# The dilated-group attention stage of a decoder step, unrolled and with plain fp32 matmuls for scores and values

## The chip, the cores and the metric

The kernel runs on one core of one Trainium2 chip. The metric is the device time of one execution in microseconds (us). Most executions of this kernel agree within 0.3%.

## The reference, cut to what matters

One step of a decoder trunk with two layers: a prompt of 2048 tokens of width 1024 and eight sample rows. Layer 0 is a gated short convolution beside attention to a memory; layer 1 is attention with three dilated windows beside attention to a memory. All is float32. The change touches the three dilated windows of the prompt. For each group (window 128 with stride 1, 512 with stride 4, 2048 with stride 16), four heads of 128 columns:

```
qb = to_res(q)                 # tokens regrouped by residue mod d, in blocks of 128
kk = with_prev(to_res(k))      # previous block and own block
vv = with_prev(to_res(v))
s = einsum('brnqhe,brnkhe->brnhqk', qb, kk)
s = where(valid, s, NEG)       # banded and causal inside the two blocks
m = max(s); p = exp(s - m); l = sum(p)
o = einsum('brnhqk,brnkhe->brnqhe', p / l, vv)
```

The kernel stores the unnormalised sums, the maxima and the denominators per group; the output stage combines the three groups with them.

## The kernel before, in words

The program is a chain of stages, each ended by a barrier: `mix_stage` and `out_stage` for layer 0, then `shared_stage` (the projections to shared keys and values, queries and gates), `dil_stage` (the three groups) and `out_stage` for layer 1. In most stages a product of two fp32 tensors is made by `split3` (L107): each operand is kept as a high part (rounded to fp32r) and a low part (the rest), and three fp32r matmuls high x high (L109), high x low (L110) and low x high (L111) accumulate in PSUM.

`dil_stage` (L3060) goes over 48 tiles: three groups of 16 blocks of 128 queries, first the group of stride 16, then 4, then 1. A tile handles the four heads. With stride 16 every residue has a single block of keys, so each of its 16 tiles has one key block. With stride 4 the first block of each of the four residues has one, the other 12 tiles have two (the previous and its own). With stride 1 tile 32 has one and the other 15 have two. In all 21 tiles have one key block and 27 have two.

The work of a tile s is spread over steps, and every engine has its own order inside a step (`body`), written by hand:

- SP (L3177): loads q and k of tile s (4 buffers each, a slot is free when the tile four back was turned), then v of tile s - 1 (`load_v`, L3171).
- TensorE (`body`, L3461): `score` of tile s - 1, `turn` of tile s (four transpositions of q into PSUM bank 0 at L3429, four of k into bank 5 at L3432), `sums` of tile s - 3 (probabilities times values), `turn_probs` of tile s - 2 (L3457).
- ScalarE (L3260): copies the high part of the turned probabilities of s - 3 (L3254, two halves), copies the sums of s - 4 (L3247), copies the high parts of the turned q and k of s (L3267, L3268), exponentials of s - 1 (L3239).
- VectorE (L3341): low parts of the probabilities of s - 3 (L3322), adds the low half of the sums of s - 4 into the output (L3330), minima of s - 1 (scaled, masked scores with a running minimum, L3312), low parts of q and k of s (L3344, L3346).
- GpSimd (L3214): splits v of s into high and low (L3220, L3222; the low part sits beside the high part, so that one 256-column matmul gives both products), then issues the stores of the denominators of s - 2 (L3167) and the output of s - 4 (L3163).

`score` waits for both low parts of the turned q and k of its tile, so the chain turn, high copy, low subtraction, score stands between one turn and the next. `turns` (L3089) emits four bodies for the first four tiles of a group and a hardware loop with four bodies for the remaining twelve; `cnt`, `half_cnt` and `use` turn a tile into semaphore values. After the last tile, the stage already begins the first tile of the output stage: SP loads its rows (L3194 to L3199), TensorE turns its query (L3477) and makes its scores by `split3`, VectorE combines the groups (`next_groups_max` to `next_combine`).

In the decode part of the output stage a plain fp32 matmul (no fp32r) stands at L2328: eight weight columns by 512 columns, 24 times in the program, and at L2326 four times by 128 columns.

Of the kernel before, what the change touches and what calls it, by code (L numbers as in the profile page):

```python
# [3059 lines left out]
def dil_stage(core, q_src, kv_src, dst, front, ahead, ops_out):  # L3060
# [11 lines left out]
    def has_prev(g, q, u):  # L3072
        d = STRIDES[g]
        if NT // d == 1:
            return False
        if d > 1:
            return u > 0
        return not (isinstance(q, int) and q == 0 and u == 0)

    def rows(ap, g, q, u):  # L3080
        d = STRIDES[g]
        view = ap.rearrange("(m d) c -> d m c", d=d)
        if NT // d == 1:
            return view[ds(q * U + u, 1), :, :].rearrange("o m c -> (o m) c")
        if d > 1:
            return view[ds(q, 1), u * P:(u + 1) * P, :].rearrange("o m c -> (o m) c")
        return view[:, ds(q * (U * P) + u * P, P), :].rearrange("o m c -> (o m) c")

    def turns(eng, body):  # L3089
        for g in range(GROUPS):  # L3090
            for u in range(U):
                body(g, 0, u)
            with eng.Fori(1, TURNS) as q:
                for u in range(U):
                    body(g, q, u)

    def back(s, k):
        g, q, u = s
        if u >= k:
            return g, q, u - k  # L3100
        if isinstance(q, int) and q == 0:
            return (g - 1, TURNS - 1, u - k + U) if g else None
        return g, q - 1, u - k + U

    END = (GROUPS - 1, TURNS, 0)

    def cnt(s, per=1, extra=1):
        g, q, u = s
        return q * (U * per) + ((g * NT + u) * per + extra)

    def half_cnt(s, half):
        return cnt(s, 2, half + 1)

    def use(s, per=16):
        return s[1] * per + (s[0] * TURNS + 1) * per

    with ExitStack() as st:
        q_b, k_b, v_b = front.dil
        o_b, lse = front.o, front.lse
        o_out, l_out = front.o_out, front.l_out  # L3120
        qt_hi = core.sb(st, "dil_qthi", [P, C], F32R)
        qt_lo = core.sb(st, "dil_qtlo", [P, C], F32R)
        kt_hi = core.sb(st, "dil_kthi", [P, H, 2, P], F32R)
        kt_lo = core.sb(st, "dil_ktlo", [P, H, 2, P], F32R)
        v_hl = core.sb(st, "dil_vhl", [P, U, H, 2, HD], F32R)
        prob = core.sb(st, "dil_prob", [P, 2, H, 2, P])
        pt_hi = core.sb(st, "dil_pthi", [P, H, 2, P], F32R)
        pt_lo = core.sb(st, "dil_ptlo", [P, H, 2, P], F32R)
        zeros = core.sb(st, "dil_zeros", [P, C])
        scratch = core.sb(st, "dil_scratch", [P, 2 * U])  # L3130
        masks = core.sb(st, "dil_masks", [P, 3 * P])
        names = ("qk_in0 qk_in1 qk_in2 qk_in3 v_in0 v_in1 v_in2 v_in3 "
                 "zeroed masked turned qhi_done khi_done qlo_done klo_done vhi_done "
                 "vlo_done scored biased exped pturned phi_done plo_done summed o_begun o_done")
        sems = core.sems(st, "dil", names)
        qk_in, v_in = (sems[n * U:(n + 1) * U] for n in range(2))
        (zeroed, masked, turned, qhi_done, khi_done, qlo_done, klo_done, vhi_done, vlo_done, scored, biased, exped, pturned,
         phi_done, plo_done, summed, o_begun, o_done) = sems[2 * U:]
        block = st.enter_context(nc.Block())

        def keys(s):

            return (1 - s[2] % 2, s[2] % 2) if has_prev(*s) else (s[2] % 2,)

        def span(s):
            ks = sorted(keys(s))
            return ks[0], ks[-1] + 1

        def mask(s):
            if has_prev(*s):  # L3150
                return masks[:, 0:2 * P] if s[2] % 2 else masks[:, P:3 * P]
            return masks[:, P:2 * P]

        scores = ps[:, 1:3, :].rearrange("p a (b s k) -> p (a b) s k", b=2, s=2)
        sums_hl = ps[:, 6:8, :].rearrange("p a (b x e) -> p (a b) x e", b=2, x=2)
        turned_p = ps[:, 3:5, :].rearrange("p a (b s k) -> p (a b) s k", b=2, s=2)
        next_q = ps[:, 0, :].rearrange("p (h t) -> p h t", h=H)
        cstat = front.cstat
        groups = lambda n: cstat[:, n, :].rearrange("p (g h) -> p g h", h=H)

        def store(eng, s, landed=None):
            eng.wait_ge(o_done, cnt(s))
            eng.dma_start(rows(dst[s[0]][:, 0:C], *s), o_b[:, s[2], :]).then_inc(landed or o_out[s[2]], 16)  # L3163

        def store_lse(eng, s, landed=None):
            eng.wait_ge(exped, half_cnt(s, 1))
            eng.dma_start(rows(dst[s[0]][:, C:OW], *s), lse[:, s[2], :]).then_inc(landed or l_out[s[2]], 16)  # L3167

        @block.sync
        def _(sp):  # L3170
            def load_v(s):  # L3171
                g, _, u = s
                if back(s, U):
                    sp.wait_ge(vlo_done, cnt(back(s, U)))
                sp.dma_start(v_b[:, u, :], rows(kv_src[g][:, C:2 * C], *s)).then_inc(v_in[u], 16)

            def body(*s):  # L3177
                g, _, u = s
                if back(s, U):
                    sp.wait_ge(turned, cnt(back(s, U)))  # L3180
                sp.dma_start(q_b[:, u, :], rows(q_src[g], *s)).then_inc(qk_in[u], 16)
                sp.dma_start(k_b[:, u, :], rows(kv_src[g][:, 0:C], *s)).then_inc(qk_in[u], 16)
                if back(s, 1):
                    load_v(back(s, 1))
            turns(sp, body)
            load_v(back(END, 1))
            sp.wait_ge(turned, NT * GROUPS)
            sp.wait_ge(vlo_done, NT * GROUPS)
            for slot in range(U):
                sp.wait_ge(o_out[slot], 16 * ((GROUPS - 1) * TURNS + 1))  # L3190
                sp.wait_ge(l_out[slot], 16 * ((GROUPS - 1) * TURNS + 1))
# [8 lines left out]
            store_lse(sp, back(END, 1), front.last_out)  # L3200
            for k in (2, 1):
                store(sp, back(END, k), front.last_out)

        @block.gpsimd
        def _(pool):
            pool.memset(zeros[:, :], 0.0).then_inc(zeroed, 1)
            pool.memset(masks[:, :], 0.0).then_inc(zeroed, 1)
            pool.wait_ge(zeroed, 2)
# [4 lines left out]

            def body(*s):  # L3214
                u = s[2]
                pool.wait_ge(v_in[u], use(s))
                if back(s, 3):
                    pool.wait_ge(summed, cnt(back(s, 3)))
                v, zero = (t.rearrange("p (h e) -> p h e", h=H) for t in (v_b[:, u, :], zeros[:, :]))
# [3 lines left out]
                if back(s, 2):  # L3223
                    store_lse(pool, back(s, 2))
                if back(s, 4):
                    store(pool, back(s, 4))
# [6 lines left out]
        def _(act):  # L3233
# [9 lines left out]
            def copy_sums(s):  # L3243
                act.wait_ge(summed, cnt(s))
                if back(s, U):
                    act.wait_ge(o_out[s[2]], use(back(s, U)))
# [376 lines left out]
```

## Time and profile before

| | us |
|---|---|
| median of 3 runs | 2947.7 |
| lowest, highest run | 2941.38, 2948.47 |
| span of the profiled execution, first to last instruction | 2951.0 |

The profiled execution's own time is given by its span alone, 3.3 us above the median of the runs. Busy shares over the span: TensorE matmuls 96%, weight loads 78%, VectorE 63%, ScalarE 40%, GpSimd 16%. Matmuls are pipelined: a record of a matmul lasts longer than the distance to the next start, so work on TensorE is costed by the distance between starts, and a merged row (x4, x8) covers from the first start to the last end. The mean granted clock of TensorE is 0.981 of 2.4 GHz; 0.50 in a row is the 1.2 GHz level. Times in the trace count from the first instruction of the span. Kernels of other stages use the same lines L109 to L111, so groups are told apart by the tiles they read and write.

### The profile page before, as it was taken

How to read it: one execution, taken by the hardware profiler on the slowest of the kernel's cores; microseconds unless marked ns; L12 is line 12 of the kernel's file. 1: busy time of each engine (PE TensorE's matmuls, PEld its weight loads, DVE VectorE, ACT ScalarE, POOL GpSimd, SP SyncE). 2: the span in 40 equal slices, each digit the busy share in tenths (PEclk: the TensorE clock that was granted, in tenths of full speed). 3: DMA queues.
4: the chain of work that ended last, by engine and by line, in shares of the span. 5: the costliest groups of instructions: out<-in, count | busy, mean ns of one | idle time of the engine just before them, and what ended most of it. 6: DMA issues, size and time to landing. Idle time of an engine off the chain costs nothing. (4 is left out here: it accounts for less than half of the span.)

```text
span 2951.0 us, 40709 instructions
## 1 busy us (share of the span) xinstructions
PE 2819.4 (96%) x13910; PEld 2315.7 (78%) x13910; DVE 1855.2 (63%) x3966; ACT 1187.9 (40%) x3494; POOL 461.8 (16%) x614
## 2 busy tenths in 40 slices
PE   7999999999998999979999999999999979989999
PEld 6787888888776888868778788777777768887787
DVE  4585766666785543334656667665746658877765
ACT  5432221312243242234343536323223458866642
POOL 0001010101000000000110202323331157640000
PEclk9999999999998999989999999999999989999999
DMA  4285645555675343232565667887776756646542
GB/s 170 84 251 192 191 154 185 183 171 178 219 243 169 108 150 107 72 133 101 192 241 194 238 203 249 258 276 223 262 250 222 266 194 210 199 145 226 198 145 98
DMA packets 281059, 556.96 MB, mean 189 GB/s; under 512 B 30385, under 2 KB 80113, under 8 KB 280873
## 3 DMA queue, kind: packets, MB, share of 16 engines
q1 hardware_dynamic: 248552, 455.99, 47.2%
q0 software_dynamic: 32320, 98.60, 9.7%
q8 instruction: 103, 1.69, 0.2%
q14 instruction: 84, 0.68, 0.1%
HBM read 421.76 MB, written 132.72 MB: 188 GB/s over the span
## 5 line engine op out<-in xcount | busy, mean ns | idle before, releaser
L109 PE MATMUL ps<-b_wp,b_sring 128*128 128x512 f32 x640 | 252.5, 395 | 17.8 <-DMA b_sring<-sums_dram 13.9
L110 PE MATMUL ps<-b_wp,b_sring 128*128 128x512 f32 x640 | 251.5, 393 | 0.0
L111 PE MATMUL ps<-b_wp,b_sring 128*128 128x512 f32 x640 | 251.5, 393 | 0.0
L109 PE MATMUL ps<-a_sring,a_wp 128*128 128x512 f32 x512 | 199.9, 390 | 2.2 <-DMA a_sring<-sums_a_dram 2.2
L111 PE MATMUL ps<-a_sring,a_wp 128*128 128x512 f32 x512 | 199.4, 389 | 0.0
L110 PE MATMUL ps<-a_sring,a_wp 128*128 128x512 f32 x512 | 199.4, 389 | 0.0
L908 DVE TENSOR_TENSOR shared_o<-ps,b_spare 128x512 f32<-128x512 f32 x160 | 109.8, 687 | 133.9 <-PE ps L111 114.9
L111 PE MATMUL ps<-b_wp,b_xtlo 128*128 128x512 f32 x496 | 193.2, 389 | 0.0
L109 PE MATMUL ps<-b_wp,b_xthi 128*128 128x512 f32 x480 | 186.9, 389 | 0.5 <-ACT b_spare L852 0.5
L110 PE MATMUL ps<-b_wp,b_xthi 128*128 128x512 f32 x480 | 186.8, 389 | 0.0
L669 POOL DMA_DIRECT2D kv_dram<-shared_o x102 | 56.3, 552 | 748.0 <-DVE shared_o L893 605.9
L713 ACT ACTIVATE ps<-shared_o 128x128 f32<-128x128 f32 (+1 forms) x408 | 108.0, 265 | 148.5 <-DVE shared_o L908 144.5
L109 PEld LDWEIGHTS ps<-b_wp,b_sring 128*128 128x128 f32 x640 | 121.6, 190 | 48.8 <-issue 15.8
L109 PE MATMUL ps<-a_xthi,out_cathi 128*128 128x512 f32 x384 | 154.5, 402 | 1.7 <-DVE out_catlo L2790 1.7
L111 PE MATMUL ps<-a_xthi,out_catlo 128*128 128x512 f32 x384 | 150.4, 392 | 0.0
L110 PE MATMUL ps<-a_xtlo,out_cathi 128*128 128x512 f32 x384 | 150.1, 391 | 0.0
L110 PE MATMUL ps<-a_xtlo,a_wp 128*128 128x512 f32 x384 | 149.5, 389 | 0.0
L111 PE MATMUL ps<-a_xthi,a_wp 128*128 128x512 f32 x384 | 149.5, 389 | 0.0
L109 PE MATMUL ps<-a_xthi,a_wp 128*128 128x512 f32 x384 | 149.5, 389 | 0.0
L111 PEld LDWEIGHTS ps<-b_wp,b_sring 128*128 128x128 f32 x640 | 121.4, 190 | 25.7
L110 PEld LDWEIGHTS ps<-b_wp,b_sring 128*128 128x128 f32 x640 | 121.4, 190 | 25.1
L893 DVE SCALAR_TENSOR_TENSOR shared_o<-shared_o,shared_stat,shared_grow 128x128 f32<-128x128 f32 (+1 forms) x408 | 122.7, 363 | 3.6
(492 smaller groups left out, 7528.9 us busy)
## 6 DMA issues: line engine op xcount, KB each, us to landing
b_sring<-sums_dram SPq DMA_DIRECT2D x160, 512.0 KB, 5.1
a_sring<-sums_a_dram SPq DMA_DIRECT2D x128, 512.0 KB, 5.0
b_raws<-w_b_dram SPq DMA_DIRECT2D x176, 256.0 KB, 4.0
a_raws<-w_a_dram SPq DMA_DIRECT2D x140, 256.0 KB, 4.3
kv_dram<-shared_o POOLq DMA_DIRECT2D x96, 256.0 KB, 4.0
tok_b_dram<-shared_o POOLq DMA_DIRECT2D x96, 256.0 KB, 4.7
front<-tok_b_dram SPq DMA_DIRECT2D x96, 256.0 KB, 3.2
front<-kv_dram SPq DMA_DIRECT2D x96, 256.0 KB, 4.1
```

The costliest lines, as they stand in the source:

```text
L109: pe.matmul(acc, a_hi, b_hi, start=first, stop=False)
L110: pe.matmul(acc, a_hi, b_lo, start=False, stop=False)
L111: return pe.matmul(acc, a_lo, b_hi, start=False, stop=last)
L669: pool.dma_start(dst, o[0:n, i % RING, :]).then_inc(o_out[i % RING], 16)
L713: sq = act.activation(to[:, cols], of[:, cols], ACT.Square, accum_out=stat[0:n, slot, 0, h:h + 1])
L893: m = dve.scalar_tensor_tensor(out=o[0:n, slot, cols], in0=of[:, cols], scalar=stat[0:n, slot, 2, h:h + 1], in1=grow[0:n, g, cols], op0=AL ...
L908: dve.tensor_tensor(o[:, i % RING, :], product, with_acc, ALU.add).then_inc(o_done if kinds[i] == "copy" else added, 1)
```

## The change

The stage is written out: 48 tiles in Python, numbered 0 to 47, with constants for all semaphore values, no hardware loop. In it:

- The turned q is copied to SBUF once, as plain fp32, by ScalarE (`copy_query`, 2 slots), the turned k once by VectorE (`copy_keys`, 3 slots), the turned probabilities of heads 0 and 1 by ScalarE (`probs_first`) and of heads 2 and 3 by VectorE (`probs_second`). Values are used as loaded, in 8 buffers of their own.
- `score` is one fp32 matmul per head, over 128 or 256 columns, in place of three fp32r; `sums` one fp32 matmul over 128 columns per head and key block, in place of two fp32r over 256 and 128.
- GpSimd computes nothing but the masks, and issues the stores. VectorE no longer adds sums: ScalarE's copy gives the output, from a PSUM bank that alternates by tile.
- The order: scores two steps behind the turn (one before), probabilities turned three behind (two before), sums four behind (three before). The scores also wait for the minima of the tile before, and turning for the copies of the tile before.

The diff, cut to its core, in this order: sizes, buffers, SP's loads, GpSimd's value operations, the orders of ScalarE and of VectorE, a score, a sum, the order of TensorE:

```diff
-    U = 4
-    TURNS = NT // U
+    U, V, R = 4, 8, 3
+    TILES = NT * GROUPS
...
+        v_b = core.sb(st, "dil_v", [P, V, C])
+        qt = core.sb(st, "dil_qt", [P, 2, C])
+        kt = core.sb(st, "dil_kt", [P, H, R, P])
+        pt = core.sb(st, "dil_pt", [P, H, 2, P])
...
+            for s in range(TILES):
+                if s >= U:
+                    sp.wait_ge(turned, s - U + 1)
+                sp.dma_start(q_b[:, s % U, :], rows(q_src, s)).then_inc(qk_in[s % U], 16)
+                sp.dma_start(k_b[:, s % U, :], rows([x[:, 0:C] for x in kv_src], s)).then_inc(qk_in[s % U], 16)
+                if s >= V:
+                    sp.wait_ge(summed, s - V + 2)
+                sp.dma_start(v_b[:, s % V, :], rows([x[:, C:2 * C] for x in kv_src], s)).then_inc(v_in[s % V], 16)
...
-                pool.tensor_tensor(v_hl[:, u, :, 0, :], v, zero, ALU.add).then_inc(vhi_done, 1)
-                pool.wait_ge(vhi_done, cnt(s))
-                pool.tensor_tensor(v_hl[:, u, :, 1, :], v, v_hl[:, u, :, 0, :], ALU.subtract).then_inc(vlo_done, 1)
...
+            for s in range(TILES + 2):
+                if real(s - 4):
+                    probs_first(s - 4)
+                if real(s - 5):
+                    copy_sums(s - 5)
+                if real(s - 2):
+                    exps(s - 2, 0)
+                    exps(s - 2, 1)
+                if real(s):
+                    copy_query(s)
...
+            for s in range(TILES + 2):
+                if real(s - 4):
+                    probs_second(s - 4)
+                if real(s - 2):
+                    minima(s - 2, 0)
+                    minima(s - 2, 1)
+                if real(s):
+                    copy_keys(s)
...
+                pe.wait_ge(q_copied, s + 1)
+                pe.wait_ge(k_copied, s + 1)
+                if s:
+                    pe.wait_ge(biased, 2 * s)
...
-                    m = split3(pe, scores[:, h, a:b, :].rearrange("p s k -> p (s k)"), qt_hi[:, cols], qt_lo[:, cols],
-                               kt_hi[:, h, a:b, :].rearrange("p s k -> p (s k)"),
-                               kt_lo[:, h, a:b, :].rearrange("p s k -> p (s k)"), True, True)
...
+                    m = pe.matmul(scores[:, h, 0:n, :], qt[:, s % 2, cols], kt[:, h, at, :], start=True, stop=True)
...
-                        pe.matmul(sums_hl[:, h, :, :].rearrange("p x e -> p (x e)"), pt_hi[:, h, key, :],
-                                  v_hl[:, slot, h, :, :].rearrange("p x e -> p (x e)"), start=(j == 0), stop=False)
-                        m = pe.matmul(sums_hl[:, h, 0, :], pt_lo[:, h, key, :], v_hl[:, slot, h, 0, :],
-                                      start=False, stop=last)
+                        m = pe.matmul(sums_at(s)[:, h, :], pt[:, h, i, :], v_b[:, key % V, cols], start=(i == 0),
+                                      stop=(i == len(order(s)) - 1))
...
+            for s in range(TILES + 2):
+                if real(s - 2):
+                    score(s - 2)
+                if real(s):
+                    turn(s)
...
+                if real(s - 4):
+                    sums(s - 4)
+                if real(s - 3):
+                    turn_probs(s - 3)
```

## Rows read from the trace of the kernel before

**Rows 1.** The head of the page.

```profile
span 2951.0 us, 40709 instructions
```

**Rows 2.** TensorE's timeline (start us, length us): turns of tiles 0, 5, 18, 47; output stage.

```profile
2373.69 0.69 PE L3429 MATMUL ps<-ident,front 128*128 128x128 f32 x2 [8.73 <-DMA front<-kv_dram]
...
2403.60 0.29 PE L3429 MATMUL ps<-ident,front 128*128 128x128 f32 x1
...
2462.60 0.60 PE L3429 MATMUL ps<-ident,front 128*128 128x128 f32 x4
...
2617.21 0.60 PE L3429 MATMUL ps<-ident,front 128*128 128x128 f32 x4
...
2641.94 1.09 PE L2915 MATMUL ps<-ident,front_od 128*128 128x128 f32 x4 [4.14 <-PEq L3117]
```

**Rows 3.** Windows: length, busy PE, PEld, DVE, ACT, POOL, clock, DMA share, GB/s.

```profile
2374.00:2386.00 12.00, 7.72 (x36) 6.97 (x34) 3.59 (x14) 4.66 (x12) 7.54 (x6) 0.50 0.84 290
2404.00:2460.00 56.00, 49.32 (x400) 44.30 (x398) 44.01 (x192) 44.69 (x159) 44.09 (x50) 1.00 0.71 227
2537.00:2617.00 80.00, 75.84 (x640) 72.91 (x640) 65.68 (x225) 66.91 (x195) 52.32 (x58) 1.00 0.53 172
```

**Rows 4.** TensorE's timeline over one period of a one-block tile.

```profile
2424.87 0.30 PE L109 MATMUL ps<-dil_kthi,dil_qthi 128*128 128x128 f32 x1 [0.57 <-DVE dil_ktlo L3346]
...
2426.24 0.62 PE L3429 MATMUL ps<-ident,front 128*128 128x128 f32 x4
...
2427.28 0.36 PE L3446 MATMUL ps<-dil_vhl,dil_pthi 128*128 128x256 f32 x1
...
2428.23 0.61 PE L3457 MATMUL ps<-ident,dil_prob 128*128 128x128 f32 x4
2429.40 0.30 PE L109 MATMUL ps<-dil_kthi,dil_qthi 128*128 128x128 f32 x1 [0.56 <-DVE dil_ktlo L3346]
```

**Rows 5.** Waits from 2404 to 2460: total us, times, longest.

```profile
PEld ps L109 <- DVE dil_qtlo L3344: 9.2, 12, 0.8
```

**Rows 6.** Groups of 2376 to 2640 by form: count | busy us, mean ns | idle before.

```profile
L3268 ACT ACTIVATE dil_kthi<-ps 128x512 fp32r<-128x512 f32 x48 | 28.4, 592 | 0.0
L3254 ACT ACTIVATE dil_pthi<-ps 128x256 fp32r<-128x256 f32 x42 | 13.5, 374 | 0.0
L3322 DVE TENSOR_TENSOR dil_ptlo<-ps,dil_pthi 128x256 fp32r<-128x256 f32 x42 | 15.9, 420 | 20.8 <-ACT dil_pthi L3254 20.8
L3330 DVE TENSOR_TENSOR dil_o<-ps,dil_o 128x512 f32<-128x512 f32 x48 | 32.9, 686 | 0.1
L3220 POOL TENSOR_TENSOR dil_vhl<-front,dil_zeros 128x512 fp32r<-128x512 f32 x48 | 61.1, 1274 | 76.5 <-PE ps L3448 71.4 <-DMA front<-kv_dram 5.1
```

**Rows 7.** Plain fp32 matmuls of the decode part (L2328, L2326) beside fp32r matmuls.

```profile
L2328 PE MATMUL ps<-b_spare,dec_sel x24: 592/592/596, 2715.7 to 2848.2; 128*8 128x512 f32 x24
...
2715.70 1.88 PE L2328 MATMUL ps<-b_spare,dec_sel 128*8 128x512 f32 x4
...
2770.65 0.39 PE L109 MATMUL ps<-b_xthi,out_cathi 128*128 128x512 f32 x1
2770.89 0.40 PE L110 MATMUL ps<-b_xtlo,out_cathi 128*128 128x512 f32 x1
...
2772.40 1.04 PE L2326 MATMUL ps<-dec_nv,ident 32*8 32x128 f32 x8
```

**Rows 8.** TensorE's timeline in a two-block step: first sums, probabilities, next scores.

```profile
2618.22 0.35 PE L3446 MATMUL ps<-dil_vhl,dil_pthi 128*128 128x256 f32 x1
...
2620.10 1.05 PE L3457 MATMUL ps<-ident,dil_prob 128*128 128x128 f32 x8
2620.90 0.37 PE L109 MATMUL ps<-dil_kthi,dil_qthi 128*128 128x256 f32 x1
```

**Rows 9.** DMA of 2400 to 2450: GB/s in 40 equal slices, and the mean.

```profile
GB/s 7 252 326 70 164 306 324 57 246 377 216 138 259 333 115 173 343 321 30 259 362 195 164 282 375 25 215 369 256 12 123 328 347 97 167 369 244 202 249 372
DMA packets 5889, 11.34 MB, mean 227 GB/s; under 512 B 1031, under 2 KB 1031, under 8 KB 5886
```

More of the change, by code:

```diff
@@ L3080, in rows @@
[L3080 to L3115, printed above, removed]
+        return g, d, NT // d, w // (NT // d), w % (NT // d)
@@ L3139, in dil_stage, with order, key_slots @@
         block = st.enter_context(nc.Block())
[L3141 to L3147, printed above, removed]
+        def order(s):
+            if not has_prev(s):
+                return [s]
+            return [s - 1, s] if s % R else [s, s - 1]
+        def key_slots(s):
+            own = s % R
+            if not has_prev(s):
+                return slice(own, own + 1)
+            return slice(own - 1, own + 1) if own else slice(0, R, R - 1)
@@ L3177, in body @@
[L3177 to L3187, printed above, removed]
@@ L3273, in _ @@
-            turns(act, body)
-            one, two, three, four = (back(END, k) for k in (1, 2, 3, 4))
-            probs(three)
-            copy_sums(four)
-            exps(one, 0)
-            exps(one, 1)
-            probs(two)
-            copy_sums(three)
+                act.wait_ge(summed, s + 1)
+                if s >= U:
+                    act.wait_ge(o_out[s % U], 16 * (s // U))
+                act.activation(o_b[:, s % U, :].rearrange("p (h e) -> p h e", h=H), sums_at(s), ACT.Copy
+                               ).then_inc(o_done, 1)
@@ L3301, in minima @@
             def minima(s, half):
-                a, b = span(s)
-                u, slot = s[2], s[2] % 2
-                if half == 0 and back(s, U):
-                    dve.wait_ge(l_out[u], use(back(s, U)))
-                dve.wait_ge(scored, half_cnt(s, half))
+                u, n = s % U, len(order(s))
+                if half == 0 and s >= U:
+                    dve.wait_ge(l_out[u], 16 * (s // U))
+                dve.wait_ge(scored, 2 * s + half + 1)
                 dve.memset(scratch[:, 2 * u + half:2 * u + half + 1], 0.0)
@@ L3327, in add_sums @@
-            def add_sums(s):
-                o = o_b[:, s[2], :].rearrange("p (h e) -> p h e", h=H)
-                dve.wait_ge(o_begun, cnt(s))
-                dve.tensor_tensor(o, sums_hl[:, :, 1, :], o, ALU.add).then_inc(o_done, 1)
-            def attend(s):
-                one, three, four = (back(s, k) for k in (1, 3, 4))
-                for half in range(2 if three else 0):
-                    probs_low(three, half)
-                if four:
-                    add_sums(four)
-                for half in range(2 if one else 0):
-                    minima(one, half)
@@ L3390, in _ @@
             dve.wait_ge(masked, 3)
[L3391 to L3397 removed]
+            for s in range(TILES + 2):
[6 more added lines that the diff above has]
+                    copy_keys(s)
             dve.wait_ge(front.qhi_done, 1)
             dve.tensor_tensor(ops_out.qt_lo, next_q, ops_out.qt_hi, ALU.subtract).then_inc(front.qlo_done, 1)
+            probs_second(TILES - 2)
+            next_groups_max()
             next_weights()
[L3401 to L3403 removed]
+            probs_second(TILES - 1)
             next_maxima()
             next_combine()
[L3406 removed]
             dve.wait_ge(front.exped, 1)
@@ L3487, in _ @@
             m.then_inc(front.scored, 1)
-            sums(one)
+            sums(TILES - 1)
 def build(nc, io):
```

240 lines of the change are left out of this document (86 added, 154 removed).

## The prediction

> **What bounds the kernel now.** The page gives the span, 2951.0 us [rows 1]; the sum is made against it, and it stands 3.3 us above the median of the runs, 2947.7. TensorE is busy nearly throughout, so I look only at the stage that the diff touches, and ask where TensorE waits there. The stage runs from the first transposition of a query at 2373.69 to the first TensorE instruction of the output stage at 2641.94, 268.3 us [rows 2]. The busy times by stretch [rows 3] show three regimes. The first tiles run at the granted clock 0.50 (the 1.2 GHz level), with TensorE busy 7.7 of 12 us. From 2404 to 2460 (group of stride 16, one key block per tile) the clock is 1.00 (2.4 GHz), yet TensorE is busy 49.3 of 56 us. From 2537 (stride 1, two blocks) it is busy 75.8 of 80.
>
> The chain of the one-block tiles is read from TensorE's timeline [rows 4]: scores at 2424.87, turning at 2426.24, sums at 2427.28, turning of probabilities at 2428.23, next scores at 2429.40. The period is 4.53 us, of which 0.57 is a wait for the low half of the keys. The waits say the same of the low half of the queries: 9.2 us in 12 waits [rows 5]. So here the latency turn, high half, low half, score sets the period. In two-block tiles it is mostly TensorE's own work.
>
> **The change, part by part.** A tile keeps its loads and its transpositions. Two things change: the arithmetic of scores and sums, and the order.
>
> *Copies.* ScalarE loses the high half of the keys (592 ns) and one of two copies of probabilities (374 ns in one-block tiles); VectorE loses the low half of the queries, one of two subtractions on probabilities (420) and the addition to the output (686); GpSimd loses both value operations (1274 for the first, about the same for the second) [rows 6]. In one-block tiles ScalarE was busy 44.7/56 x 4.53 = 3.6 us per tile [rows 3] and keeps 3.6 - 0.6 - 0.4 = 2.6, VectorE falls from 3.6 to about 1.8. I cost both at nothing, hidden beside TensorE. In two-block tiles they were busy 66.9 and 65.7 of 80 us and only lose work, so TensorE covers them. If it did not, ScalarE would be next, with the copy of the queries queued behind the exponentials; that copy is needed only at the turn after next score, some 4.5 us after a score begins against 7 (two-block).
>
> *Order.* Scores come two steps behind the turn instead of one, sums four behind, probabilities three. The wait of 0.57 goes. New waits: the scores wait for the minima of the tile before (VectorE ends them about 2.8 us into a two-block iteration of 5.5), turning waits for the copies of the tile before. Both are over before TensorE comes. SP loads v behind q and k of its tile and waits for sums seven tiles back; q and k of the next tile stand behind that wait, but those sums ran three steps before. GpSimd's queue issues the two stores, now with no compute ahead of them; they have about four iterations to land. Nothing there costs time.
>
> *Price of a plain fp32 matmul.* This form does not stand in the stage. The nearest rows are in the decode part [rows 7]: 24 matmuls of the program over 512 columns with eight weight columns are 48 records (24 on this tile, 24 on another), and four records start within 1.88 - 0.59 = 1.29 us, 0.43 each; for 128 columns, eight records take 1.04 - 0.27 = 0.77, 0.110 each. So one program matmul is two records, each of two cycles a column: 0.213 us for 256 columns, 0.107 for 128. The unknown is the load of 128 weight columns instead of 8. A lower bound is those values. For an upper bound without surprise: eight fp32 transpositions, each with a fresh 128-column load, take 0.80 us [rows 8], and 16 fp32r matmuls of the sums 1.88, 0.1175 each: 0.120 and 0.228. I take 0.113 and 0.222, near the transpositions, since they too load full fp32 weights.
>
> The Trainium skill, "FP8 and Floating Point Precision", TensorE Precision Notes, says that true fp32 makes four passes through the array where fp32r makes one. This speaks against the change, which puts four passes in place of three in the scores. The rows agree with it over 512 columns (0.86 us against 0.24 from one fp32r start to the next [rows 7]). What it would do to short matmuls is the slow case below.
>
> *One tile on TensorE.* Two blocks: scores 8 records x 0.222 + 0.08 at the seam = 1.86; turn 1.01 (2617.21 to 2618.22); sums 16 x 0.113 + 0.05 = 1.86; probabilities 0.80; sum 5.53. Before it was 5.2 plus waits; a little is lost here. One block: 8 x 0.113 + 0.08 = 0.98; 1.03; 0.95; 0.44; sum 3.40, against 4.53.
>
> *Stretches.* (A) Turn 0 to turn 5 took 29.9 us (2373.69 to 2403.60 [rows 2]). After: five turns, four scores, two of probabilities and one of sums, at half clock 9 + 7.2 + 1.7 + 1.8 = 19.7 without a gap; 16.2 if the clock rises around tile 3, as the array is busy without pause sooner. I take 18: gain 11.9 (10.1 to 13.7). (B) Turn 5 to turn 18 took 59.0 (to 2462.60), 13 x 4.53. TensorE would allow 3.40. But a tile moves 1.05 MB: at 3.40 that is 308 GB/s. Between 2400 and 2450 it was 227 on the mean, with slices up to 375 [rows 9]. I take 3.6 us (292 GB/s): gain 13 x 0.93 = 12.1 (0 at the mean rate of before, 14.7 at 3.40). (C) Turn 18 to turn 47 took 154.6 (to 2617.21). After: scores of 25 two-block and 4 one-block tiles 50.4, turns 29.3, sums (22 and 7) 47.6, probabilities (23 and 6) 21.0, together 148.3: gain 6.3 (2.0 to 10.7 by the bounds of the price, over 200 and 440 records). (D) Turn 47 to the output stage took 24.7. After: the rest of step 47 3.6, step 48 4.6; then scores 1.9, next query 0.4, sums and probabilities 2.7, a wait of 0.3 for ScalarE's copy, the same again 2.7, the next stage's twelve fp32r scores 1.5; then on VectorE maxima 1.4, combination and gate 3.0, and 2.0 for handing over (I estimate these three from the same work of before): 15.9. Together 24.1: gain 0.6 (-0.5 to 1.5).
>
> Sum: 11.9 + 12.1 + 6.3 + 0.6 = 30.9, a span of 2920.1 us and a median of 2916.8.
>
> **The rivals.** *The loads are not hidden (slow side).* If the load of 128 fp32 weight columns does not pass beside the matmul, a record costs 0.214 and 0.32. C becomes 148.3 + 440 x 0.101 + 200 x 0.098 = 212.3, a loss of 58; B 5.0 a tile, a loss of 6; D a loss of 9; A still gains 4: 69 us slower, 3017. If instead each of four passes pays what an fp32r pass pays (0.11 at 128, 0.12 at 256 columns), a matmul costs 0.44 and 0.48, C loses 44, B 7, D 8, A gains 6: 53 slower, 3001. The second price is what the rule of four passes gives by itself, in the Trainium skill's page named above. For it: at 128 columns an fp32r pass already takes what a weight load takes (twelve in 1.37 us [rows 4]), so passes could not get cheaper. Against it: only two loads per matmul are recorded, and transpositions hide theirs. The point from which it decides is 0.035 us more per record: 736 records in C and D and 208 in B eat 30.9. Chance 0.12. *Half of it:* a record costs about 0.15 and all is given back: within 0.3%, 2947; chance 0.09.
>
> *DMA holds the one-block tiles.* The gaps of before hide a transfer rate near what the queues give; a tile stays at 4.5 us, now with TensorE waiting for q and k. B gains nothing: 30.9 - 12.1 = 18.8, a median of 2928.9. For it: a busy share of 0.71 already, 0.84 at the start [rows 3]. Against it: slices at 375. Chance 0.15, and faster all the same.
>
> *The change does not do what it says:* the written-out bodies stall on fetching code and the loops' latency comes back elsewhere. Against it: the output stage's sixteen steps are written out too. Chance 0.02, slower.
>
> **How the numbers follow.** Forecast 0.62, DMA 0.15, given back 0.09, slow 0.14 together. The forecast's own range by the bounds: 2947.7 - 40.6 = 2907 to 2947.7 - 11.6 = 2936. Eight in ten: 2905 to 2944, leaving out the slow cases and about half of the given-back one. Faster by over 0.3% (9 us, about what a measurement of this kernel can tell from no change) 0.77; within it 0.09; slower 0.14.
>
> **What would show it.** In the profile after: two MATMUL records per program matmul, starts 0.11 and 0.22 apart; turns 3.6 us apart in the stride-16 group, and near 5.5 in the stride-1 group, slightly longer than before; no wait of the scores for VectorE; TensorE's busy share near 95% after the first tiles; ScalarE under 85%. Starts 0.15 apart or more would make the price wrong; a wait for the kv loads in the stride-16 group would speak for DMA; the clock below 1.00 past 2393 would make A wrong.

## The result, and the profile after

| | before | after |
|---|---|---|
| median, us | 2944.5 (4 runs, 2937.0 to 2948.5) | 2893.6 (4 runs, 2891.2 to 2894.6) |
| span of the profiled execution, us | 2951.0 | 2892.8 |
| ratio of the times | | 0.984, 95% interval 0.982 to 0.985 |

The medians differ by 51.0 us (the ratio and its interval give 48, between 44 and 52); forecast were 30.9, from a median of three runs that stood 3.2 higher, and 2893.6 lies below the range's low end of 2905. The head of the page of after, which answers to [rows 1]:

```profile
span 2892.8 us, 38889 instructions
## 1 busy us (share of the span) xinstructions
PE 2789.1 (96%) x13718; PEld 2294.2 (79%) x13718; DVE 1781.2 (62%) x3822; ACT 1147.9 (40%) x3398; POOL 341.3 (12%) x517
```

TensorE's share is 96% as before: a mean over all stages says nothing here. The starts of turns do. TensorE's timeline of after at the points of [rows 2] (turn of tile 0, tile 5, tile 18 just behind the scores shown, tile 47, output stage); columns are start, length:

```profile
2366.54 1.11 PE L3344 MATMUL ps<-ident,front 128*128 128x128 f32 x4 [8.65 <-DMA front<-kv_dram]
...
2381.58 0.60 PE L3344 MATMUL ps<-ident,front 128*128 128x128 f32 x4
...
2421.84 0.60 PE L3344 MATMUL ps<-ident,front 128*128 128x128 f32 x4
...
2562.24 0.60 PE L3344 MATMUL ps<-ident,front 128*128 128x128 f32 x4
...
2585.30 0.63 PE L2915 MATMUL ps<-ident,front_od 128*128 128x128 f32 x4 [3.70 <-PEq L3086]
```

The stretches, from such rows:

| us | A: turn 0 to 5 | B: 5 to 18 | C: 18 to 47 | D: 47 to output stage | stage | one-block, two-block period |
|---|---|---|---|---|---|---|
| before | 29.9 | 59.0 | 154.6 | 24.7 | 268.3 | 4.53; 5.16 and 5.66 in turn |
| forecast | 18 | 46.8 | 148.3 | 24.1 | 237.2 | 3.6; 5.53 |
| after | 15.0 | 40.3 | 140.4 | 23.1 | 218.8 | 3.10; 5.26 |

The stage gives 49.5 us. From its end to the end of the span the two profiled executions differ by 1.6 more (309.1 and 307.5), but that is no gain of the change: the repeat of after below has 308.9 there, and before with its loops written out 306.0. The spans differ by another 7.2 ahead of the first turn (2373.69, 2366.54), where the code is the same in all kernels shown here; over their profiled executions the first turn starts anywhere from 2363.3 to 2374.0. The profiled execution of before was a long one of its kernel. So the stage explains the 51.0 of the medians to within the spread between executions.

Windows of after, answering to [rows 3] (length, busy PE, PEld, DVE, ACT, POOL, granted clock, DMA share, GB/s):

```profile
2366.00:2374.00 8.00, 5.92 (x27) 5.52 (x28) 2.12 (x11) 2.52 (x4) 0.00 (x0) 0.50 1.01 345
2374.00:2378.00 4.00, 3.65 (x31) 3.49 (x30) 2.49 (x17) 3.90 (x18) 0.58 (x1) 0.95 1.06 394
...
2385.00:2421.00 36.00, 36.00 (x328) 36.00 (x327) 24.30 (x140) 33.52 (x130) 12.46 (x23) 1.00 0.96 328
...
2524.00:2562.00 38.00, 38.00 (x287) 36.08 (x286) 21.42 (x87) 26.02 (x79) 7.94 (x15) 1.00 0.47 161
```

In both groups (strides 16 and 1) TensorE shows no idle time at all. The granted clock stands near the 2.4 GHz level from some 8 us into the stage; in the same view of before it stayed at 0.50 for 22:

```profile
2374.00:2396.00 22.00, 16.47 (x75) 15.35 (x74) 7.61 (x38) 8.61 (x26) 8.13 (x7) 0.50 0.59 201
2396.00:2404.00 8.00, 7.48 (x58) 6.94 (x58) 5.73 (x20) 6.93 (x26) 5.62 (x6) 0.91 0.59 196
```

The steps themselves: TensorE's timeline of after, one one-block step and one two-block step:

```profile
2411.66 1.06 PE L3333 MATMUL ps<-dil_kt,dil_qt 128*128 128x128 f32 x8
2412.55 0.60 PE L3344 MATMUL ps<-ident,front 128*128 128x128 f32 x4
2412.99 0.60 PE L3349 MATMUL ps<-ident,front 128*128 128x128 f32 x4
2413.42 1.06 PE L3361 MATMUL ps<-dil_v,dil_pt 128*128 128x128 f32 x8
2414.32 0.60 PE L3370 MATMUL ps<-ident,dil_prob 128*128 128x128 f32 x4
...
2557.85 1.95 PE L3361 MATMUL ps<-dil_v,dil_pt 128*128 128x128 f32 x16
2559.63 1.04 PE L3370 MATMUL ps<-ident,dil_prob 128*128 128x128 f32 x8
2560.51 1.89 PE L3333 MATMUL ps<-dil_kt,dil_qt 128*128 128x256 f32 x8
2562.24 0.60 PE L3344 MATMUL ps<-ident,front 128*128 128x128 f32 x4
```

No row has a wait in brackets, unlike [rows 4]. From start to start: eight records over 128 columns 0.89 (0.111 each), a turn 0.87, sixteen records 1.78 (0.111), eight transpositions of probabilities 0.88 (0.110), eight records over 256 columns 1.73 (0.216). So a plain fp32 matmul is two records of just over 0.107 and 0.213 us, the lower bounds of the forecast: the loads of the weights add nothing to them.

Against [rows 4] the one-block period fell by 1.43 us, in two halves. 0.73 of it lies between the turning of the probabilities and the next scores (1.17 before, 0.44 after), where the wait stood. The other 0.70 is TensorE's own: scores 1.37 to 0.89 (twelve records to eight), turn 1.04 to 0.87, sums 0.95 to 0.90. Over the 13 periods of B that is 9.5 and 9.1 us.

### The profile page after: what moved, and what is told of

It reads as the page before. It is cut to its first block and busy times, and to the rows that moved or that the text cites. A ratio compares the mean times of both kernels' runs of the same rounds, so it can differ in the third digit from the quotient of the medians.

```text
span 2892.8 us, 38889 instructions
## 1 busy us (share of the span) xinstructions
PE 2789.1 (96%) x13718; PEld 2294.2 (79%) x13718; DVE 1781.2 (62%) x3822; ACT 1147.9 (40%) x3398; POOL 341.3 (12%) x517
## 5 line engine op out<-in xcount | busy, mean ns | idle before, releaser
L109 PE MATMUL ps<-b_wp,b_sring 128*128 128x512 f32 x640 | 251.9, 394 | 16.4 <-DMA b_sring<-sums_dram 12.1
```

Source lines behind the costliest of these rows:

```text
L109: pe.matmul(acc, a_hi, b_hi, start=first, stop=False)
```

## The experiments

Nine runs beside the pair itself. The theory: in one-block tiles the chain from the turn over high and low copies to the scores set the period, and single copies take it away. The rivals: the greater distances in the order do it, or the written-out loops do, or TensorE's own work, to which half of the one-block gain belongs by the rows above.

**The loops alone.** The kernel before with `turns` in Python:

```diff
-            for u in range(U):
-                body(g, 0, u)
-            with eng.Fori(1, TURNS) as q:
+            for q in range(TURNS):
                 for u in range(U):
                     body(g, q, u)
```

> The kernel before with its hardware loops written out, everything else as it was. Theory (the loops cost nothing): the median stays within 3 us of the kernel before, and the stage (first transposition to the output stage's first TensorE instruction) at 268 us, one-block turns still 4.53 us apart. Rival (the loops are what cost): 5 to 15 us faster, with the gain at each fourth tile, where a loop turns round.

Measured: 2943.2 us, ratio 0.9999 (0.9989 to 1.0009); the stage 266.6 us, stretches 28.6, 59.0, 154.4, 24.6. The loops cost nothing that can be measured. TensorE's timeline of it, two scores of following tiles:

```profile
2427.84 0.30 PE L109 MATMUL ps<-dil_kthi,dil_qthi 128*128 128x128 f32 x1 [0.56 <-DVE dil_ktlo L3344]
...
2432.37 0.30 PE L109 MATMUL ps<-dil_kthi,dil_qthi 128*128 128x128 f32 x1 [0.56 <-DVE dil_ktlo L3344]
```

The period of 4.53 and the wait of 0.56 are those of [rows 4].

**The old order with the new arithmetic.** The changed kernel with scores one step behind the turn, probabilities two, sums three, on each engine. ScalarE's copy of q also stands ahead of the exponentials again, as the high halves did before; the cut shows TensorE's part:

```diff
-                if real(s - 2):
-                    score(s - 2)
+                if real(s - 1):
+                    score(s - 1)
...
-                if real(s - 4):
-                    sums(s - 4)
-                if real(s - 3):
-                    turn_probs(s - 3)
+                if real(s - 3):
+                    sums(s - 3)
+                if real(s - 2):
+                    turn_probs(s - 2)
```

> The kernel after with the step distances of before (scores one step behind the turn, probabilities two, sums three); plain fp32 throughout. Theory A (the greater distance took the wait away, as the prediction had it): one-block turns 3.5 to 4.0 us apart instead of 3.10, the stage 6 to 14 us longer than the kernel after's 218.8. Theory B (one plain copy each on two engines makes the chain short enough by itself): one-block turns at most 3.2 apart, the stage within 3 us of 218.8.

Measured: 2896.7 us, ratio 0.985 (0.983 to 0.986); stage 219.6. TensorE's timeline of it, one period in the stride-16 group:

```profile
2412.94 1.06 PE L3333 MATMUL ps<-dil_kt,dil_qt 128*128 128x128 f32 x8
2413.84 0.60 PE L3344 MATMUL ps<-ident,front 128*128 128x128 f32 x4
2414.27 0.60 PE L3349 MATMUL ps<-ident,front 128*128 128x128 f32 x4
2414.71 1.06 PE L3361 MATMUL ps<-dil_v,dil_pt 128*128 128x128 f32 x8
2415.60 0.60 PE L3370 MATMUL ps<-ident,dil_prob 128*128 128x128 f32 x4
2416.04 1.06 PE L3333 MATMUL ps<-dil_kt,dil_qt 128*128 128x128 f32 x8
```

3.10 without a wait, and 5.26 in two-block tiles. The distances are not what takes the chain away. They move work between the ends: A, B and C are 3.1, 0.8 and 1.3 longer (18.1, 41.1, 141.7), D 4.4 shorter (18.7).

**The scores put back, the sums plain.** High and low copies of q and k, distances as in the changed kernel:

```diff
-                act.activation(qt[:, s % 2, :], ps[:, 0, :], ACT.Copy).then_inc(q_copied, 1)
+                act.activation(qt_hi[:, s % 2, :], ps[:, 0, :], ACT.Copy).then_inc(q_copied, 1)
+                act.activation(kt_hi[:, :, s % R, :], ps[:, 5, :].rearrange("p (h k) -> p h k", h=H), ACT.Copy
+                               ).then_inc(k_high, 1)
...
-                    m = pe.matmul(scores[:, h, 0:n, :], qt[:, s % 2, cols], kt[:, h, at, :], start=True, stop=True)
+                    m = split3(pe, scores[:, h, 0:n, :], qt_hi[:, s % 2, cols], qt_lo[:, s % 2, cols],
+                               kt_hi[:, h, at, :], kt_lo[:, h, at, :], True, True)
```

> The kernel after with the scores in three fp32r matmuls again (high and low parts of queries and keys), sums in plain fp32, order of after. By the prices read in the kernel after (0.111 for a 128-column record, 0.216 for 256) against 0.111 and 0.120 of an fp32r pass: a one-block tile gets 0.44 us more on TensorE and 0.6 more on ScalarE, so turns 3.6 to 3.8 apart; a two-block step 5.26 - 0.29 = 4.97. Stage 218.8 + 10 - 8 = 221, that is 45 to 50 us faster than before. Rival (the fp32 scores carry the gain): stage 230 or more, with waits of the scores for VectorE back in it.

Measured: 2918.8 us, ratio 0.992 (0.990 to 0.994); stage 243.6 (19.6, 55.3, 145.7, 23.0); periods 4.25 and 5.21. The expectation (periods of 3.6 to 3.8 and 4.97, a stage of 221) missed; its rival's number, 230 or more, came. One part back costs 25 us, 15 of them in B alone. Waits of it from 2404 to 2450 (who waited, for what, us, times, longest), then TensorE's timeline:

```profile
DVE dil_qtlo L3264 <- ACT dil_qthi L3206: 19.5, 11, 1.8
...
PE ps L3357 <- DVE dil_qtlo L3264: 5.1, 11, 0.5
```

```profile
2426.84 0.28 PE L111 MATMUL ps<-dil_kthi,dil_qtlo 128*128 128x128 f32 x1
2427.58 0.63 PE L3357 MATMUL ps<-ident,front 128*128 128x128 f32 x4 [0.47 <-DVE dil_qtlo L3264]
```

The wait has moved. With scores two steps behind, they find their operands; now the turn waits, since PSUM bank 0 is free only when the low half of the last turned q has been read from it. ScalarE ends its exponentials at 2426.14, makes the high half, VectorE begins the low half at 2426.74 and has it 0.6 later, and the next turn starts at 2427.58. The chain goes through the bank instead of the operand. Distance in the order does not shorten it, since a turn waits for the bank of the tile just before it at any distance. The expectation had not seen this. The size of the loss belongs to this order too: ScalarE makes the high halves behind the exponentials here, ahead of them before, and no other order was tried. And part of the loss is TensorE's own: twelve fp32r records start over 1.38 us (to 2426.96, one spacing behind the last), against 0.89.

**The scores put back only in the two-block groups** (tiles 16 and up), to ask whether the plain form costs TensorE anything where the chain does not bind:

```diff
+                if s < SPLIT:
+                    act.activation(qt[:, s % 2, :], ps[:, 0, :], ACT.Copy).then_inc(q_copied, 1)
+                    return
...
+                    if s < SPLIT:
+                        m = pe.matmul(scores[:, h, 0, :], qt[:, s % 2, cols], kt[:, h, s % 2, :], start=True, stop=True)
+                    else:
+                        m = split3(pe, scores[:, h, 0:n, :], qt_hi[:, s % 2, cols], qt_lo[:, s % 2, cols],
+                                   kt_hi[:, h, at, :], kt_lo[:, h, at, :], True, True)
```

> As the kernel after in the group of stride 16, scores in three fp32r matmuls in the other two groups. Theory (TensorE's own work bounds the two-block tiles, and 3 x 0.120 is less than 2 x 0.216): two-block steps 4.97 us, 27 of them give 7.8, five one-block tiles take back 2.2: stage 213 us, median about 5 us under the kernel after's. Rival (the low halves come late and stall the scores): steps at 5.2 or more, no gain.

Measured: 2905.3 us, ratio 0.987 (0.985 to 0.989); stage 225.6, two-block tiles 5.21 where 4.97 had been expected. TensorE's timeline of one step, then VectorE's:

```profile
2550.14 0.36 PE L109 MATMUL ps<-dil_kthi,dil_qthi 128*128 128x256 f32 x1
...
2551.53 0.28 PE L111 MATMUL ps<-dil_kthi,dil_qtlo 128*128 128x256 f32 x1
2551.77 0.63 PE L3369 MATMUL ps<-ident,front 128*128 128x128 f32 x4
2552.28 0.66 PE L3374 MATMUL ps<-ident,front 128*128 128x128 f32 x4
2552.77 1.95 PE L3386 MATMUL ps<-dil_v,dil_pt 128*128 128x128 f32 x16
2554.56 1.04 PE L3395 MATMUL ps<-ident,dil_prob 128*128 128x128 f32 x8
2555.35 0.36 PE L109 MATMUL ps<-dil_kthi,dil_qthi 128*128 128x256 f32 x1
```

```profile
2550.93 0.69 DVE L3273 TENSOR_TENSOR dil_qtlo<-ps,dil_qthi 128x512 fp32r<-128x512 f32 x1 [1.93 <-ACT dil_qthi L3211]
2551.54 0.68 DVE L3275 TENSOR_TENSOR dil_ktlo<-ps,dil_kthi 128x512 fp32r<-128x512 f32 x1
```

The work is there as expected: twelve score records need 12 x 0.126 = 1.51 (0.38 a head, the plain form 0.43). But TensorE reaches the turn before VectorE has read bank 0: the low half of q ends at 2551.62 and the turn starts at 2551.77, 0.24 behind the last score instead of 0.12; the low half of k ends at 2552.22 and its transpositions start at 2552.28, 0.51 behind the first instead of 0.43. So 0.24 of the 0.29 that the split should have saved a step (5.26 - 4.97) is lost again to waits, in steps where I had thought VectorE early. In the stride-4 group, where one-block tiles are mixed in, they cost more: turn 18 to turn 32 takes 68.8 us against 64.5 in after; turn 32 to 47 takes 77.0 against 75.9. The rival is right.

**Records of 64 columns,** to find what holds a record, stream or weight load. Each sum in two halves over the columns; twice as many records over half as many columns:

```diff
+                    for part in range(2):
+                        half = slice(h * HD + part * 64, h * HD + part * 64 + 64)
...
+                            m = pe.matmul(sums_at(s)[:, h, part * 64:part * 64 + 64], pt[:, h, i, :],
+                                          v_b[:, key % V, half], start=(i == 0), stop=(i == len(order(s)) - 1))
```

> The kernel after with every fp32 matmul of the sums cut into two over 64 columns each, same weights, so 1200 records in place of 600. If a record over 128 columns is held by its stream (two cycles a column), a record over 64 costs 0.053 to 0.06 and the stage stays at 218.8 within 5 us. If the load of 128 weight columns sets a floor of 0.107 to 0.11, each record still costs that: 600 x 0.11 = 66 us more on TensorE, the stage 275 to 290.

Measured, in a single run: 2953.5 us; stage 281.9, 63.1 more than after; periods 3.94 and 7.00. TensorE's timeline of it:

```profile
2411.57 1.90 PE L3363 MATMUL ps<-dil_v,dil_pt 128*128 128x64 f32 x16
2413.31 0.61 PE L3372 MATMUL ps<-ident,dil_prob 128*128 128x128 f32 x4
```

1.74/16 = 0.109 us a record, as much as over 128 columns: the stream does not hold it. A fixed distance between any two records is not it either. Before has eight transpositions of 8 rows in its decode part, at the clock of 1.00:

```profile
2869.68 0.41 PE L2336 MATMUL ps<-ident,dec_dilog 8*128 8x8 f32 x4
2869.95 0.39 PE L2336 MATMUL ps<-ident,dec_memog 8*128 8x8 f32 x4
```

Each loads 8 rows of 128 weight columns, and they start 0.27/4 = 0.068 us apart. So in this kernel a record that loads full weights, 128 rows by 128 columns, does not start more often than every 0.11 us; which part of the load sets this (rows, or the form) was not tried apart. At 128 columns the price by stream (0.107) and the one by load (0.109) are nearly equal; below, the load decides. So the forecast's price for 128 columns came out near its lower bound, and with 64 columns the gain of the whole change is given back.

**An unused load of v per tile,** to ask whether DMA is near its limit. It goes into a buffer that nothing reads, for the first 16 tiles. The repeat of after ran beside it.

```diff
+                if s < NT:
+                    if s >= U:
+                        sp.wait_ge(x_in[s % U], 16 * (s // U))
+                    sp.dma_start(x_b[:, s % U, :], rows([x[:, C:2 * C] for x in kv_src], s)).then_inc(x_in[s % U], 16)
```

> The kernel after with one more load of v per tile in the group of stride 16 (into a buffer that nothing reads): 1.31 MB a tile instead of 1.05. If the DMA engines were near their limit at 3.10 us a tile (339 GB/s), as slices of 375 in the kernel before suggest, turns go to 3.5 to 3.7 us apart and TensorE waits for q and k: 6 to 10 us more. If there is room (the rate could rise to 423 GB/s), turns stay at 3.10.

> The kernel after once more, for the spread of stretches between executions: the stage at 218.8 within 1 us, one-block turns 3.10 apart, two-block steps 5.26; the stretch ahead of the stage anywhere between 2366 and 2374.

Measured, in a single run each: 2895.6 and 2893.2 us; stages 221.5 and 218.7 (the latter 15.0, 40.3, 140.4, 23.1, after to a tenth). DMA of after from 2385 to 2425, then of the kernel with the extra load:

```profile
DMA packets 6829, 13.26 MB, mean 331 GB/s; under 512 B 1189, under 2 KB 1189, under 8 KB 6822
```

```profile
DMA packets 8187, 15.83 MB, mean 396 GB/s; under 512 B 1342, under 2 KB 1342, under 8 KB 8181
```

A third more loads (256 KB beside 768 a tile), 396 GB/s, and 8 of 13 periods in B stay within 0.06 of 3.10, five lie at 3.18 to 3.86 (all B 42.2 against 40.3). So 331 GB/s left room for 65 more, and at 396 TensorE begins to wait for its loads (0.8 us in two waits in B). A period of 3.10 throughout would have taken 423 GB/s by the expectation; every slice of this stretch lies between 371 and 420, so the queues are probably near what they give here. The expectation named neither this rate nor the mixed outcome.

**The sums put back, the scores plain.** The mirror of the run with split scores: values split by GpSimd (into five slots, as memory allowed), high and low probabilities, fp32r sums in one pair of PSUM banks in place of two that alternate, the addition on VectorE. Values are loaded into four buffers, behind q and k of the next tile; the last run below shows that this order of loads alone changes nothing in B:

```diff
+                    pool.tensor_tensor(v_hl[:, s % W, :, 0, :], v, zero, ALU.add).then_inc(vhi_done, 1)
...
-                act.activation(pt[:, 0:2, 0:n, :], turned_p[:, 0:2, 0:n, :], ACT.Copy).then_inc(first_done, 1)
+                for half in range(2):
+                    heads = slice(2 * half, 2 * half + 2)
+                    act.wait_ge(pturned, 2 * s + half + 1)
+                    act.activation(pt_hi[:, heads, 0:n, :], turned_p[:, heads, 0:n, :], ACT.Copy).then_inc(phi_done, 1)
...
+                dve.tensor_tensor(o, sums_hl[:, :, 1, :], o, ALU.add).then_inc(o_done, 1)
...
+                        pe.matmul(sums_hl[:, h, :, :].rearrange("p x e -> p (x e)"), pt_hi[:, h, i, :],
+                                  v_hl[:, key % W, h, :, :].rearrange("p x e -> p (x e)"), start=(i == 0), stop=False)
```

> The changed kernel with the sums alone put back: GpSimd splits the values again, ScalarE copies the high half of the turned probabilities, VectorE subtracts the low half and adds the low sums into the output, 8 or 16 fp32r matmuls; scores stay plain, order and distances stay. Theory (the gain comes from the copies between turn and score, the plain sums bring little but their own records): one-block tiles 3.1 + 0.06 for the sums + about 0.2 for two changes of form = 3.4 us, two-block tiles 5.26 + 0.09 + 0.1 = 5.4 to 5.5; stage near 232 us, median near 2906. Rival (the copies behind the probabilities and the addition behind the sums hold the one-block tiles just as the low halves of q and k do): one-block 3.9 us or more with waits of the sums for dil_ptlo or dil_vhl or for the output, stage 240 or more, median 2914 or more. If scores and sums were independent parts, 25.3 for the scores (measured) would leave about 24 for this part together with order and loops, and the median would be 2917.

Measured: 2936.0 us, ratio 0.998 (0.997 to 0.999); stage 260.6 (14.9, 56.5, 158.8, 30.5), periods 4.34 and 5.69. The theory's 2906 was 30 us off; the rival's waits came, and the times lie well above the rival's lower bounds: one part back gives up 42 of the 49 us. TensorE's timeline, then VectorE's, then ScalarE's of the same 5 us:

```profile
2415.77 0.60 PE L3384 MATMUL ps<-ident,front 128*128 128x128 f32 x4
2417.01 0.35 PE L3396 MATMUL ps<-dil_vhl,dil_pthi 128*128 128x256 f32 x1 [0.64 <-POOL dil_vhl L3191]
```

```profile
2415.47 0.76 DVE L3277 TENSOR_TENSOR dil_ptlo<-ps,dil_pthi 128x256 fp32r<-128x256 f32 x2 [1.43 <-ACT dil_pthi L3219]
2416.22 0.69 DVE L3285 TENSOR_TENSOR dil_o<-ps,dil_o 128x512 f32<-128x512 f32 x1
```

```profile
2415.59 0.59 ACT L3211 ACTIVATE dil_o<-ps 128x512 f32<-128x512 f32 x1
2417.38 0.40 ACT L3203 ACTIVATE dil_prob<-dil_prob,dil_lse 128x128 f32<-128x128 f32 x1 [1.19 <-DVE dil_lse L3266]
```

The sums wait 0.64. The trace names GpSimd's split, but that ended at 2416.54, half a microsecond early; what ends at 2416.84 to 2416.91, just before 2417.01, is VectorE's addition, which empties the only pair of banks and for which these sums wait in the code. No run took the addition away alone. It is part of a circle between ScalarE and VectorE, read from the starts: high probabilities 2415.07, copy of the sums 2415.59, addition 2416.22, minima 2416.84, exponentials 2417.38, copy of q 2418.93, high probabilities again 2419.41. That is 4.34, TensorE's period, while TensorE was busy only 80% from 2390 to 2430. How much of this the hand-made order of this kernel causes (no other order was tried) stays open.

**v behind q and k of the next tile,** an attempt to do better than after, whose tile 1 waits 1.54 us for its q and k. The edit is in SP's order alone (v of s - 1 after q and k of s):

```diff
-                if s >= V:
-                    sp.wait_ge(summed, s - V + 2)
-                sp.dma_start(v_b[:, s % V, :], rows([x[:, C:2 * C] for x in kv_src], s)).then_inc(v_in[s % V], 16)
+                if s:
+                    load_v(s - 1)
```

> The changed kernel with one edit: SP issues the load of v of tile s-1 behind q and k of tile s, as the kernel before did, so that the first turns get their q and k sooner. Theory (the fill still waits 1.5 us for the q and k of tile 1 behind v of tile 0): the first five turns 1 to 1.5 us shorter, the rest unchanged, median 1 us lower, which these rounds cannot tell from none. Rival (the transfers of the fill share the queues anyway): the same time, the wait moves to tile 2 or 3.

Measured: 2895.7 us, ratio 0.984 (0.982 to 0.986). A is 14.2 instead of 15.0, the stage 217.9; the time cannot be told from that of after. Nothing tried here beats the changed kernel.

## Why the prediction was wrong in size

**What the miss is made of.** The stage gained 49.5 us where 30.9 were forecast, 18.6 more. The step that failed most is the forecast's sum of TensorE's work in a tile, 3.40 and 5.53 us, where 3.10 and 5.26 were measured with TensorE never idle: 3.9 us in B and 7.9 in C, mainly because a pause in the turn and the seams were counted as work that stays. The DMA term in B is 2.6 us, A with its early clock 3.0, D 1.1. The remaining 1.5 us of the medians lie outside the stage, within the spread.

**The mechanism held, with one attribution wrong.** The forecast had the chain turn, high, low, score set the one-block period, and it is gone. But it said under *Order* that scores two steps behind make the wait of 0.57 go. The old distances with single copies run at 3.10, and the new distances with split scores at 4.25. What takes the chain away is the single copy, which frees operand and PSUM bank at once. The prediction costed what happens to the copies at nothing and gave the order the credit; it was the reverse. (The run with split scores differs from before in ScalarE's order and in its plain sums too, so that distance alone is useless is shown less firmly than that the copy alone suffices.)

**It is not the sum of its parts.** With the scores split the stage is 24.8 us longer than after, with the sums split 41.8, together 66.6, more than the whole gain of 49.5. Either part left alone holds the one-block tiles near their old 4.53 (4.25, 4.34), by a chain of its own; in the orders tried here, only without both does TensorE set the period. The forecast looked for the wait that ends last ([rows 5]) and did not ask what the next one would give.

**B: 18.7 instead of 12.1.** Two terms failed. "I take 3.6 us (292 GB/s)" put 0.20 us a tile on TensorE's 3.40 for DMA, 2.6 of the 6.6 us. The stretch ran at 3.10 us with 328 GB/s and moved 396 with a load added. The mean of 227 in [rows 9] was what the tiles asked for, not what the queues give; the slices of 375 in the same row said so. The larger part, 13 x 0.30 = 3.9 us, is the sum of 3.40 itself, which measured 3.10: the seams (0.08 and 0.05) and the turn (1.03 against 0.87).

**C: 14.2 instead of 6.3**, beyond the bound of 10.7. The step that failed is the sum 5.53 for a two-block tile; it measured 5.26:

| term, us | forecast | after |
|---|---|---|
| scores | 8 x 0.222 + 0.08 = 1.86 | 1.73 |
| turn | 1.01 | 0.87 |
| sums | 16 x 0.113 + 0.05 = 1.86 | 1.78 |
| probabilities | 0.80 | 0.88 |

The turn was taken from [rows 2, 8] as work, yet 0.15 of its 1.01 is a pause ahead of the first fp32r sum (0.58 from the second transpositions to it; 0.43 to a plain sum in after), which the waits put down to issue. The 0.05 for a seam in the sums is not there. The 0.08 in the scores and the short 0.80 of the probabilities cancel: the first fp32r record behind transpositions is shown 0.08 early (0.80 behind them and 0.20 ahead of the second record, where plain records stand 0.88 behind and fp32r records 0.12 apart). The prices per record were 2 to 3% high. With the four measured terms the forecast's own counts give 46.8 + 25.2 + 45.4 + 22.9 = 140.3 for C, where one-block terms are 0.89 and 0.44. The clause "slightly longer than before" had the right comparison with TensorE's work (5.21 from 2615.69 to 2620.90 before, 5.26 after) and left out that TensorE stood idle 4.2 of 80 us in [rows 3]: those tiles took 5.16 and 5.66 in turn. Of the 14.2 us, 8.9 came from turn 18 to 32 (73.4 to 64.5), where one-block tiles are mixed in.

**A: 14.9 instead of 11.9**, beyond 13.7. The bound took the clock's rise around tile 3; the granted clock is 0.95 from 2374 on, at tile 2, with TensorE busy 5.9 of the 8 us before. Why it rose so much sooner than before was not tried by itself, so this part of the gain is luck as far as the forecast goes. That the array is busy without pause sooner, as the forecast had it, does not explain it alone: with split scores TensorE was busy 10.0 of the 10 us from 2378 to 2388, from 4 us into the stage on, and the granted clock was 0.50 in them. In all runs with single copies for these tiles A is 14.2 to 18.1, with split sums, which only come in at the end of A, 14.9, and with split scores 19.6. Turns of after start 3.50, 3.47, 2.72, 2.23 and 3.12 us apart, and in the run with old distances A is 18.1. **D: 1.7 instead of 0.6**, presumably the same lower prices of records; it was not taken apart.

**The slow case did not come.** Records start 0.111 and 0.216 apart, 0.004 and 0.003 above the lower bounds; its deciding point was 0.035 more a record. The Trainium skill ("FP8 and Floating Point Precision", TensorE Precision Notes) names four passes for true fp32. If each cost what an fp32r matmul takes, a plain one over 128 columns would cost 0.44; the trace has 0.222, and three fp32r matmuls 0.34 (1.37 for twelve in [rows 4]), so at 128 columns plain is the cheaper form on TensorE. Over 256 columns three fp32r matmuls take 0.38 a head and the plain one 0.43: there the rule's direction holds, its size (four against three) does not. The case that the change does not do what it says is ruled out by the loops alone at 0.9999.

**Of what was to be shown:** starts 0.11 and 0.22 apart came; 3.6 and 5.5 did not (3.10, 5.26); no wait of the scores came; TensorE was at 100% rather than 95; the clock was early. ScalarE, forecast under 85%, was busy 33.5 of 36 us, 93%: 2.9 us of each 3.10, where 2.6 had been forecast. The forecast took off the lengths of the records, 592 and 374 ns, but ScalarE's records overlap as well: in before they start 0.48 and 0.26 apart, and 3.6 - 0.48 - 0.26 is 2.9. ScalarE would be next if TensorE's part shrank.

**The range** ended at 2905 because even its best case kept the seams and the long turn (B at 3.40 a tile) and half the clock up to tile 3. With B at 40.3 and C at 140.3 in the forecast's sum the gain is 11.9 + 18.7 + 14.3 + 0.6 = 45.5, a median of 2902.

## What to carry to other kernels

Before a split into high and low copies is costed by its matmuls, follow who waits for the low half, as operand and as reader of the PSUM bank: here TensorE's own work in a two-block step did not shrink (5.21 to 5.26 us), and in a one-block tile half of the 1.43 us gained was a wait for copies that the plain form does not need. A mean transfer rate in a stretch that waits for something else is a demand, not a limit. And when a chain is removed, work out the period that the next chain would give, part by part; with two chains of nearly equal length, removing one gave 8 us (plain scores alone) or 25 us (plain sums alone), both together 49.5.

## What was not expected of the hardware

- A record that loads 128 rows by 128 columns of weights takes 0.109 to 0.111 us at the clock of 1.00 whether 64 or 128 columns of fp32 stream past; with two records a matmul, a plain fp32 matmul with such weights did not go below 0.22 us. Records that load 8 rows of 128 columns start 0.068 apart.
- Between four transpositions and the first fp32r sum stand 0.58 us, in one- and two-block tiles of before and with the loops written out (2425.14 to 2425.71), between the same transpositions and a plain sum 0.43. The trace says issue; the cause was not tried.
- The queues moved 396 GB/s on the mean over 40 us, with slices from 371 to 420, beside a TensorE that hardly waited (0.8 us).
